# The start of a hybrid decoder layer: load order, transposes tile by tile, and where the constants queue

## What is computed

```python
def token_mix(x, pool_prev, mem_k, mem_v, pos0, w_in, b_in, ln_v_g, ln_v_b, w_s, b_s, ...):
    proj = x @ w_in + b_in
    z = jax.nn.gelu(proj[..., :OFF_P])
    u, v = z[..., :A_WIDTH], z[..., A_WIDTH:]
    ...
    v = layer_norm(v, ln_v_g, ln_v_b)
    mixed = spatial_gating(v.reshape(...), w_s, b_s)
    br_a = (u * mixed.reshape(N, L, A_WIDTH)) @ w_a_out
    ...
    h = gates[:, :, 0] * br_a + gates[:, :, 1] * br_b + gates[:, :, 2] * br_m
    return h @ w_o, p_ext[:, -POOL_HIST:], v

def expert_block(args):          # 32 experts, each token goes to 4
    xb, e = args
    h = xb @ w1[e] + b1[e]
    g = jnp.minimum(h[:, :D_FF], SWIGLU_LIMIT)
    lin = jnp.clip(h[:, D_FF:], -SWIGLU_LIMIT, SWIGLU_LIMIT)
    act = g * jax.nn.sigmoid(SWIGLU_ALPHA * g) * (lin + 1.0)
    return act @ w2[e] + b2[e]
```

## Time and profile before

| what | value |
|---|---|
| median of 3 runs | 1397.7 us (1396.99 to 1398.77) |
| span of the profiled execution, first to last instruction | 1397.3 us; its device time is not listed apart |
| TensorE busy | 1317.2 us, 94% of the span |
| VectorE, ScalarE, GpSimd busy | 417.7, 244.1, 217.2 us |
| DMA | 464.79 MB, mean 333 GB/s |

### The profile page before, as it was taken

The page is one execution under the profiler, slowest core; times in us unless marked ns, Lnnn a source line. Parts: engine busy times, 40 slices in busy tenths (PEclk is TensorE's granted clock), DMA queues, the critical chain, the costliest instruction groups (busy, mean ns, idle before and its releaser), DMA issues.

```text
span 1397.3 us, 17570 instructions
## 1 busy us (share of the span) xinstructions
PE 1317.2 (94%) x6912; PEld 790.6 (57%) x6912; DVE 417.7 (30%) x782; ACT 244.1 (17%) x338; POOL 217.2 (16%) x93
## 2 busy tenths in 40 slices
PE   6999999998889999999999999999999999999994
PEld 5989889998854534444443444444344454434441
DVE  3480482286421212202121220212122131221215
ACT  3433443332210101101101010110101010010101
POOL 4546167654500000000000000000000000000001
PEclk9979999999869999999999999999999999999997
DMA  9434675742549999999999999999999999999871
GB/s 309 158 114 151 199 244 187 193 151 95 233 196 399 419 418 414 417 418 417 418 414 415 413 417 415 416 419 417 412 414 417 418 413 419 416 416 415 362 291 39
DMA packets 121209, 464.79 MB, mean 333 GB/s; under 512 B 8625, under 2 KB 47077, under 8 KB 88304
## 3 DMA queue, kind: packets, MB, share of 16 engines
q1 hardware_dynamic: 116464, 456.68, 82.7%
q0 software_dynamic: 1456, 5.11, 1.2%
q10 hardware_dynamic: 3256, 2.53, 0.7%
HBM read 461.51 MB, written 2.90 MB: 332 GB/s over the span
## 4 chain that ended last, share of the span: by engine, by line
PE 89%; DVE 4%; ACT 3%; issue 1%; ACTq 1%; POOL 1%; DVEq 0%; POOLq 0%
PE ps L1526 32%; PE ps L1558 16%; PE ps L1228 15%; PE ps L1213 12%; PE ps L1569 6%; PE ps L1239 2%; ACT actT L730 1%; PE ps L1320 1%; PE ps L1510 1%; PE ps L1329 1%; DVE ypair L1119 1%; PE ps L1533 1%; ACT xg L718 1%; POOL ring_lo L496 1%; PE ps L1306 1%
## 5 line engine op out<-in xcount | busy, mean ns | idle before, releaser
L1526 PE MATMUL ps<-ring,xg 128*64 128x512 f32 x2048 | 457.5, 594 | 0.0
L1526 PEld LDWEIGHTS ps<-ring,xg 128*64 128x64 f32 x2048 | 204.0, 137 | 221.0 <-issue 177.7
L496 POOL TENSOR_TENSOR ring_lo<-ring,w_hi 128x2048 fp32r<-128x2048 f32 x40 | 188.2, 4707 | 136.9 <-ACT w_hi L572 125.5
L1558 PE MATMUL ps<-ring,actT 128*64 128x512 f32 x768 | 171.8, 596 | 14.9 <-ACT actT L730 14.9
L539 POOL TENSOR_TENSOR yacc<-yacc,lnb 128x512 f32<-128x512 f32 x2 | 3.3, 1644 | 1006.6 <-ACT yacc L594 1006.6
L1213 PE MATMUL ps<-pick,x 128*128 128x128 f32 (+1 forms) x816 | 152.5, 318 | 1.2 <-DVE pick L1106 1.2
L1213 PEld LDWEIGHTS ps<-pick,x 128*128 128x128 f32 (+1 forms) x816 | 115.8, 196 | 57.7 <-issue 30.7
L1137 DVE TENSOR_SCALAR gm<-ps 128x512 f32<-128x512 f32 x32 | 22.1, 692 | 408.1 <-PE ps L1526 408.1
L1558 PEld LDWEIGHTS ps<-ring,actT 128*64 128x64 f32 x768 | 52.3, 137 | 112.2 <-issue 91.4
L725 ACT ACTIVATE sg<-gm 128x512 f32<-128x512 f32 x32 | 20.1, 629 | 543.4 <-DVE gm L1137 543.4
L1569 PE MATMUL ps<-ypair,pickT 128*128 128x512 f32 (+1 forms) x192 | 91.6, 611 | 14.2 <-DVE ypair L1119 14.2
(11 more groups left out here) (264 smaller groups left out, 1065.5 us busy)
## 6 DMA issues: line engine op xcount, KB each, us to landing
ring<-in_w SPq DMA_DIRECT2D x352, 1024.0 KB, 10.0
spare<-in_w SPq DMA_DIRECT2D x32, 1024.0 KB, 11.5
ring<-in_w_in SPq DMA_DIRECT2D x24, 1024.0 KB, 6.4
ring<-in_cache_mem_k SPq DMA_DIRECT2D x4, 1024.0 KB, 5.3
ring<-in_cache_mem_v SPq DMA_DIRECT2D x4, 1024.0 KB, 6.1
ring<-in_w_a_out SPq DMA_DIRECT2D x4, 1024.0 KB, 9.9
ring<-in_w_o SPq DMA_DIRECT2D x4, 1024.0 KB, 5.0
ring<-in_w_mk SPq DMA_DIRECT2D x2, 1024.0 KB, 5.3
```

The costliest lines, as they stand in the source:

```text
L496: pool.tensor_tensor(ring_lo[:, SLOTS[key] % HR, :], slot(*key), w_hi[:, SPLITS.index(key) % 2, :].bitcast(F32), ALU.subtract)\
L1526: ins = pe.matmul(ps[CAP * hh:CAP * hh + CAP, b, :], xg[:, k, par, :], ring[:, w1_slot, 512 * p:512 * p + 512], start=False, stop=(k == KD ...
L1558: ins = pe.matmul(ps[CAP * dh:CAP * dh + CAP, YB, :], actT[:, f % 4, f // 4, :], w[:, kk, 512 * dh:512 * dh + 512], start=False, stop=(f = ...
```

## The change

- SP issues x with one semaphore for each of the three tiles; behind the third slot it issues the two `bvb` transfers, behind the sixth `wsr`, `bsb`, `wpool`, `wr` and `brb`. ScalarE keeps the two of `brow`.
- ScalarE applies a GELU to six columns of the identity into `stats` (scratch there) before its copies.
- TensorE waits for the identity alone, and for x tile by tile: all eight pieces of a tile, then the next tile. The wait for the other constants comes behind the transposes.
- VectorE makes four low parts of x, then casts slot v0, then makes the other four, then writes the low part of v0's channel block 0; GpSimd writes only that of block 1. The first block's third eight matmuls wait for VectorE's half (`first_low`).

```diff
+        def channels(w, c):
+            return w.rearrange("p (k n) -> p k n", k=KD)[:, :, P * c:P * c + P]
...
             for m in range(2):
-                sp.dma_start(x[:, m, :], a["x_prompt"][P * m:P * m + P, :]).then_inc(x_in, 16)
-            sp.dma_start(x[0:64, 2, :], a["x_sample"]).then_inc(x_in, 16)
+                sp.dma_start(x[:, m, :], a["x_prompt"][P * m:P * m + P, :]).then_inc(x_in[m], 16)
+            sp.dma_start(x[0:64, 2, :], a["x_sample"]).then_inc(x_in[2], 16)
             for n, key in enumerate(slots):
...
+                if n == 2:
+                    for i, row in enumerate((a["ln_v_g"], a["ln_v_b"])):
+                        sp.dma_start(bvb[:, i, :], rows(row)).then_inc(vparam_in, 16)
+                elif n == HR - 1:
+                    sp.dma_start(wsr[:, :, :], a["w_s"].rearrange("g t s -> t g s")).then_inc(ws_in, 16)
...
-            lows(*SPLITS[at_v:at_mk])
+            pool.wait_ge(w_high, 1)
+            pool.tensor_tensor(channels(ring_lo[:, 0, :], 1), channels(ring[:, 0, :], 1),
+                               channels(w_hi[:, 0, :], 1).bitcast(F32), ALU.subtract).then_inc(w_low, 1)
+            lows(*SPLITS[at_v + 1:at_mk])
...
-            for i, src in enumerate((a["ln_v_g"], a["ln_v_b"])):
...
-            act.dma_start(brb[:, :], rows(a["b_r"])).then_inc(const_in, 16)
+            act.wait_ge(consts, 1)
+            act.activation(stats[:, 0, 0, :], ident[:, 0:6], ACT.Gelu_apprx_tanh)
...
-            dve.wait_ge(*loaded("v", 0))
-            dve.tensor_copy(w_hi[:, 0, :], slot("v", 0)).then_inc(w_high, 1)
-            for k in range(KD):
+            def x_lower(k):
                 dve.wait_ge(*full("xT", k))
                 dve.wait_ge(x_high, k + 1)
                 dve.tensor_tensor(xT_lo[:, k, :], bank("xT", k)[:, 0:T], xT_hi[:, k, :].bitcast(F32), ALU.subtract)\
                    .then_inc(*frees("xT", k))
+            for k in range(KD // 2):
+                x_lower(k)
+            dve.wait_ge(*loaded("v", 0))
+            dve.tensor_copy(w_hi[:, 0, :], slot("v", 0)).then_inc(w_high, 1)
+            for k in range(KD // 2, KD):
+                x_lower(k)
+            dve.wait_ge(w_high, 1)
+            dve.tensor_tensor(channels(ring_lo[:, 0, :], 0), channels(ring[:, 0, :], 0),
+                              channels(w_hi[:, 0, :], 0).bitcast(F32), ALU.subtract).then_inc(first_low, 1)
...
-                    pe.wait_ge(w_low if step == 2 else w_high, SPLITS.index(key) + 1)
+                    if (kind, c, step) == ("v", 0, 2):
+                        pe.wait_ge(first_low, 1)
+                    else:
+                        pe.wait_ge(w_low if step == 2 else w_high, SPLITS.index(key) + 1)
...
+            pe.wait_ge(consts, 1)
+            for tt in range(3):
+                pe.wait_ge(x_in[tt], 16)
+                for k in range(KD):
+                    ins = pe.transpose(opens("xT", k)[:, P * tt:P * tt + ROWS[tt]], x[0:ROWS[tt], tt, P * k:P * k + P],
+                                       ident[0:ROWS[tt], 0:ROWS[tt]])
+                    if tt == 2:
+                        ins.then_inc(*fills("xT", k))
             pe.wait_ge(consts, 10)
-            pe.wait_ge(x_in, 48)
-            for k in range(KD):
-                out = opens("xT", k)
-                for tt in range(3):
...
```

More of the change, by code:

```diff
@@ L247, in build @@
         bank_free = [sem(f"bank_free{i}") for i in range(8)]
-        x_in, bias_in, vparam_in, const_in, ws_in, hist_in, ln_in, b1_in, b2_in = (sem(n) for n in (
-            "x_in", "bias_in", "vparam_in", "const_in", "ws_in", "hist_in", "ln_in", "b1_in", "b2_in"))
+        x_in = [sem(f"x_in{tt}") for tt in range(3)]
+        bias_in, vparam_in, const_in, ws_in, hist_in, ln_in, b1_in, b2_in = (sem(n) for n in (
+            "bias_in", "vparam_in", "const_in", "ws_in", "hist_in", "ln_in", "b1_in", "b2_in"))
         cv_out, mkv_out, pout_out, hist_out, y_out = (sem(n) for n in (
@@ L254, in build @@
         consts, ops_pool, ops_dve = sem("consts"), sem("ops_pool"), sem("ops_dve")
+        first_low = sem("first_low")
         w_high, w_low, x_high, mem_high, a_high, a_low, o_high, yb_high, h_high, h_low = (sem(n) for n in (
@@ L382, in _ @@
                     .then_inc(slot_full[n % HR], 16)
+                if n == 2:
[3 more added lines that the diff above has]
+                    sp.dma_start(wsr[:, :, :], a["w_s"].rearrange("g t s -> t g s")).then_inc(ws_in, 16)
+                    sp.dma_start(bsb[:, :, :].rearrange("p g t -> p (g t)"),
+                                 rows(a["b_s"].rearrange("g t -> (g t)"))).then_inc(const_in, 16)
+                    sp.dma_start(wpool[:, :, :], a["w_pool"].rearrange("g c d -> c g d")).then_inc(const_in, 16)
+                    sp.dma_start(wr[:, :, :], a["w_r"].rearrange("(k p) e -> p k e", k=KD)).then_inc(const_in, 16)
+                    sp.dma_start(brb[:, :], rows(a["b_r"])).then_inc(const_in, 16)
             def load(e, par, j):
@@ L1255, in _ @@
             xT, aT, ybT, oT, hT_parts = (xT_hi, xT_lo), (aT_hi, aT_lo), (ybT_hi, ybT_lo), (oT_hi, oT_lo), (hT_hi, hT_lo)
-            pe.wait_ge(consts, 10)
-            pe.wait_ge(x_in, 48)
-            for k in range(KD):
-                out = opens("xT", k)
-                for tt in range(3):
-                    ins = pe.transpose(out[:, P * tt:P * tt + ROWS[tt]], x[0:ROWS[tt], tt, P * k:P * k + P],
-                                       ident[0:ROWS[tt], 0:ROWS[tt]])
-                ins.then_inc(*fills("xT", k))
+            pe.wait_ge(consts, 1)
[6 more added lines that the diff above has]
+                        ins.then_inc(*fills("xT", k))
+            pe.wait_ge(consts, 10)
             pe.wait_ge(bias_in, 32)
```

## The result

The changed kernel takes 1389.10 us (median of five runs, 1388.11 to 1392.81) against 1397.77 of the kernel before beside it (six runs, 1396.57 to 1401.57); the ratio is 0.9938, with an interval of 0.9924 to 0.9952. That is 8.7 us less, by the ratio (0.0062 × 1397.8) and by the medians. A sixth run of the changed kernel took 1760.48 us at a mean granted clock of 0.72 and is left out, and so are two single runs far off in the comparisons further on (4566.34 us of e2, 1431.38 of the kernel before). Two more comparisons of the same two kernels gave 0.9957 (0.994 to 0.9974) and 0.993 (0.9917 to 0.9944); over all comparisons the mean of before is 1397.95 us (46 runs) and that of the change 1390.03 (15 runs), so 7.9 us is the best value of the gain. The forecast was 1390.5.

A forecast was written before the change was run, and what follows sets the result against it. The start was taken as bound by ScalarE's issue queue until 17.02 us, then TensorE. First matmul 7.8 earlier less 0.6 for the clock gave 7.2; 1397.3 - 7.2 + 0.4 = 1390.5 us, range 1387.0 to 1395.0.

The forecast's parts named there:

- a rigid shift: Whole program: everything after the start should move with the first matmul, so a gain there is kept.
- x tile by tile: Start: transposes begin at 4.2 instead of 10.1 us, as each tile lands, and end at 9.4.
- Neither later tile is waited for: Start: tiles land at 4.2, 5.7 and 6.4; transposes reach the later two at 6.1 and 8.0 us.
- ScalarE and VectorE: Start: table load off the path, first low part 9.0, fourth done 10.65, cast to 11.9, first matmul 12.0, 7.8 earlier.
- Rival 1: Start: first slot lands late, at 12.2; first matmul 13.6, gain 5.6, time 1392.1 us; 9%.
- The low slot in two: First slot's low part: GpSimd's half 12.0 to 14.2, VectorE's ends 15.4, TensorE comes at 15.8; cover 0.4 us.
- Rival 2: Shared port: GpSimd takes it for slot 1 first, VectorE ends 20.1, TensorE stands 4.3 us; 1394.8 us; 6%.
- The constants: SP's queue: constants behind the slots all land by about 32 us, before first use; cost nothing.
- The clock of the first block: First channel block: the TensorE clock's later rise makes it 0.6 us dearer, bounds 0 to +1.2.
- 0.4 us lie around the span: Whole kernel: profiled span 1397.3 us stands for a median of 1397.7, the difference lying outside it.
- Rival 5: Clock after 80 us: the fall at 87.6 does not come, at most half of 17.1 us saved; 1382 us; 3%.
- What falls with the transposes: Start: transposes do not bring TensorE's full clock; were it otherwise, up to 1.4 us more is gained.

The follow-up runs named there:

- e2: Kernel before with only x on three semaphores and transposed tile by tile, ScalarE keeping its nine transfers; 1398.17 us, ratio 0.9998.
- e4: The changed kernel run again, unchanged, against the kernel before; 1391.32 us, ratio 0.9957.
- e7: Changed kernel, but SP issues the constants ahead of the weight slots, behind x; 1398.43 us, ratio 1.0004 to the kernel before.
- e10: Like the kernel with the halved cast (e9), but GpSimd does not wait for VectorE's half of the low slot; 1388.59 us.
- e9: Changed kernel with v0's cast halved between VectorE (after two low parts) and ScalarE, GpSimd waiting for VectorE's low half; 1388.73 us, ratio 0.9925.
- e5: Changed kernel without the split: GpSimd writes the whole low part of slot v0; 1391.76 us.
- e6: Changed kernel without the split: VectorE writes the whole low part of slot v0, GpSimd begins with slot v1; 1388.12 us.
- e11: The changed kernel a third time, unchanged, against the kernel before; 1389.02 us, ratio 0.993.
- e1: Kernel before with only the seven constants issued by SP behind the third and sixth slots; 1393.65 us, ratio 0.9978.
- e8: Changed kernel without ScalarE's early GELU on six columns of the identity; 1390.56 us.
- e3: Kernel before with constants moved and x tile by tile, but old VectorE order, no split, no early GELU; 1391.72 us, ratio 0.9961.

## Why the prediction was right, step by step

**What bounds the start, and a rigid shift: right.** The chain has only the start's steps and then TensorE. From the start of wsr to the end, before and e4, which share their clock history, take 1317.1 us both. No gain was lost on the way.

**x tile by tile: right, with one false statement.** The start of the transposes was given as 4.2 and is 4.43, their duration as 5.2 (4.2 to 9.4) and is 4.85. "Neither later tile is waited for" is wrong: PEld stood 0.30 us for the second tile, which landed near 6.2 instead of 5.7, and x_sample landed at 7.3 instead of 6.4 (issued at 1.74, 5.6 us to landing). The terms of 0.75 us for its bytes took the rate of a full queue for the first transfers. It cost nothing, since the transposes came to it only at about 8.1. The idle gap that grouping removes stands ahead of a 64-row piece (8.16), not behind it as the prediction has it; one gap of eight is left either way.

**ScalarE and VectorE: right.** First low part predicted at 9.0, measured 9.10; the fourth done at 10.65, cast from 10.70; first matmul **12.0** against 12.02. Of the two reasons given, the freed queue and the freed bandwidth, e7 shows that the first is not enough when the slot comes late, and e2 that with all nine transfers on its queue ScalarE cannot begin until 16.1, however early the transposes are done. What each is worth alone was not run. The cover was thin: the slot was to land at 9.5, a good us ahead of the cast. It landed at 10.2, 0.5 ahead, and in e10 at 11.0, after it. That the start came out at 12.02 owes something to luck, since this cover took up the 0.7 us of the late slot. Rival 1 (12.2) did not come, but its mechanism came nearer than 9% suggests.

**The low slot in two: sizes right, worth overestimated.** VectorE's half was given as ready at 13.55 and done at 15.4, and was from 13.43 to 15.47; GpSimd's as 12.0 to 14.2 and was 12.01 to 14.39. The 1.2 us from a line through two rows is 1.22 in e9. The lock of the port behaves as forecast: 2.04 beside GpSimd against 1.22 free, and further on a cast of 128 columns took 4.66 us beside GpSimd's 4.62 (15.65). The Trainium skill, SBUF — State Buffer, section "SBUF: two separate sides", states this exclusive lock, and the trace agrees. TensorE came to this step at 16.27 in the first trace and at 15.81 in e4 (15.8 predicted; the prediction counted the clock's later rise in a term of its own, but not here), so the cover was 0.8 and 0.3 us. What the prediction did not ask is whether the split is worth anything: 0.5 to 0.7 us against GpSimd alone by e5, nothing against VectorE alone by e6.

**Rival 2 had more room than thought.** The margin for VectorE was put at 0.2 us. GpSimd's next slot was ready only at 15.52 (ScalarE's cast, 13.62 plus 1.90), 1.1 us after VectorE had the port, since slot 1 landed at 13.6 instead of 12.5.

**The constants: right.** All landed by 33.5 us (32 predicted), wsr is first used at 72.9.

**The clock of the first block: right in size.** Predicted 0.6 dearer, measured 0.46 (5.42 against 4.96). 7.8 less 0.5 is the 7.3 us that wsr starts earlier.

**Two terms were wrong and nearly out of sight.** First, "0.4 us lie around the span": the changed kernel's profiled execution took 1389.1 with a span of 1387.3, so 1.8 us lie around it, and another of its runs 1388.46 with 1386.6. The profiled execution of before was thus near 1399, slower than the median it was held to stand for. The forecast did not suffer, since 1397.3 and 0.4 add up to that median. Second, the clock after 80 us was taken as fixed, apart from the rivals. It is not: one and the same kernel shows either kind of stretch, worth 2.7 us together. Rival 5 named this place, but as a fall that is missing; it came shorter, not missing. The first comparison (8.7 us) may be above the predicted 7.2 for this reason, though only one of its runs was traced; over all comparisons (7.9) little of the difference is left.

The change does not make the shorter kind by itself. Among the traces a mean granted clock of 0.975 stands only with the short kind of both stretches (first trace, e7, e11), and in the comparisons with e1 to e11 the kernel before has this mean in 12 of its 40 runs; these average 1396.1 us, all 40 of them 1397.9. Like with like, at 0.975, the change is 7.0 us faster (1389.1 in two runs against 1396.1), near the 7.3 of the start. Whether the change makes the shorter kind more frequent isn't shown: of the nine traces whose first matmul comes before 13 us four have it in both stretches, but e7, with the old start, has it too.

**What falls with the transposes.** The prediction took from 7.35 us of transposes without a rise that they don't bring the full clock. Six runs contradict it. The granted clock of e4 at the start:

```profile
10.00:12.00 2.00, 0.01 (x1) 0.00 (x0) 2.00 (x5) 1.33 (x5) 0.00 (x0) 0.90 0.98 323
12.00:14.00 2.00, 1.94 (x7) 1.97 (x8) 2.00 (x5) 0.19 (x1) 1.95 (x1) 0.50 1.09 346
14.00:16.00 2.00, 2.00 (x12) 2.00 (x12) 2.00 (x6) 1.72 (x1) 0.63 (x2) 0.75 1.11 358
```

In this trace the clock is recorded as going up to 2.4 GHz at 8.18 us, when all that TensorE had done were transposes, and down at 11.6 (the 0.90 of 10 to 12 us is 1.6 us at full and 0.4 at half level), just before the first matmul; it is back at 15.0 (0.75 of 14 to 16). Ahead of a trace's first such record the column says 1.00 whatever the level: it does so in the changed kernel's first trace from 12 to 16 us, where eight matmuls take 2.47 us that take 1.33 later. In the changed kernel's first trace the rise came at 16.07 with none before it, and so in e7, e8 and e11. The Trainium skill, TensorE: Matmul & The Clock Gate, section "Part 4: PE-mode transpose", says that transposes don't bring the full clock; e3, e4, e5, e6, e9 and e10 do not agree. What was to be gained by it, up to 1.4 us by the prediction, was at most the 0.5 us by which e4's first block is shorter (4.92 against 5.42): the clock was down again at 11.6, while TensorE waited for the cast.

## What to carry to other kernels

At a start where everything is loaded at once, put behind the first weights all that isn't needed for them, and issue it from an engine that has nothing else to do (4.9 us of the start here, both together). Only then does it pay to begin work on each tile as it lands (nothing without the first step, 2.9 us with it). An experiment that takes one of two causes away must leave the other as it was: e7 freed a queue and at once made the slot later. Before an operation is split over VectorE and GpSimd, price VectorE alone: half the columns beside GpSimd took 2.04 us, all of them alone 2.28. Hold the profiled span against the device time of its own execution, and compare the stretches of low clock of two traces before a difference of 1 to 3 us is put down to an edit.

## What the runs showed of the hardware

- The same code had stretches at the lower TensorE clock of 17.1 and 6.8 us in one execution and of 13.7 and 3.4 in two others; 2.7 us of the span hang on it.
- Float32 transposes alone were followed by the full clock at 8.1 to 8.8 us in six of the ten traces that have them in one piece from 4.3 to 4.8 us on, and not in the other four (the change in two of its three traces, e7, e8); nor in e1 or the kernel before, after 7.35 us of them.
- The first slot's landing scatters with the same order of issues: 10.1 in e9, 10.2 in the changed kernel, 11.0 in e10. A start planned to a few tenths of a us behind a transfer is not kept in each execution.
- Issues on one engine's queue hold those behind them: in e7 SP came to the first slot at 11.46, behind the constants, and it landed 6.95 us later, at 18.4; in the changed kernel it was issued at 2.38 and landed at 10.2.
